# Experts' results scaled at eviction and scattered with a DMA addition into one sum per token

## The reference, cut to what matters

```python
def _hier_moe(h, ..., w_gate, w_up, w_down):
    ...                                     # two experts and two weights for each token
    e_a = expert_id.reshape(-1)             # 4096 assignments
    tok_a = jnp.repeat(jnp.arange(t_count), EXPERT_TOPK)
    w_a = gate_w.reshape(-1)
    ...                                     # sorted by expert, each expert padded to blocks of 128
    slot_tok = jnp.zeros((n_slots,), jnp.int32).at[dest].set(tok_s)
    slot_w = jnp.zeros((n_slots,), h.dtype).at[dest].set(w_s.astype(h.dtype))
    def run_block(args):
        tok, e = args
        xb = h[tok]
        a = xb @ w_gate[e]                  # 1024 x 512
        u = xb @ w_up[e]
        return (jax.nn.silu(a) * u) @ w_down[e]   # 512 x 1024
    y = lax.map(run_block, (slot_tok.reshape(n_blocks, MOE_BLOCK), block_expert))
    y = y.reshape(n_slots, D_MODEL) * slot_w[:, None]
    return jnp.zeros((t_count, D_MODEL), h.dtype).at[slot_tok].add(y)
```

## Time and profile before

| what | value |
|---|---|
| median of three runs | 2801.63 us (2801.57 to 2801.66) |
| profiled execution, its own time | 2803.04 us |
| its span (first to last instruction) | 2801.3 us |
| granted TensorE clock, mean over the span | 0.925 of full |
| busy share of the span | PE 86%, DVE 49%, ACT 33%, POOL 17% |
| moved by DMA | 499.73 MB |
| `combine` stage (first DMA issue to the end of the span) | 2679.11 to 2801.3 us |

### The profile page before, as it was taken

How to read it: one execution, slowest core, us unless ns; L and a number is a source line. 1 busy time by engine, 2 the same in 40 slices (tenths; PEclk the granted TensorE clock), 3 DMA queues, 4 the chain that set the end, 5 groups by cost and what they waited for, 6 DMA issues and landing times. The chain is left out here.

```text
span 2801.3 us, 39203 instructions
## 1 busy us (share of the span) xinstructions
PE 2397.4 (86%) x13485; PEld 2056.7 (73%) x13486; DVE 1365.5 (49%) x1700; ACT 917.5 (33%) x1509; POOL 474.8 (17%) x311
## 2 busy tenths in 40 slices
PE   3599999999999888868959983999999999999910
PEld 3488888888888677846848873888889889889910
DVE  6552111122323177646424447886664756466346
ACT  3200000000000055433322221886664755565321
POOL 2311111111111101022335541010010100010032
PEclk9799999999999999769979995999999999999955
DMA  6112212132332423255554433998975876678468
GB/s 224 46 60 90 75 60 75 60 111 102 132 124 101 162 99 109 81 166 200 200 197 158 151 135 127 368 375 300 323 258 207 289 272 231 240 254 296 184 224 270
DMA packets 293164, 499.73 MB, mean 178 GB/s; under 512 B 21337, under 2 KB 226673, under 8 KB 283506
## 3 DMA queue, kind: packets, MB, share of 16 engines
q1 hardware_dynamic: 269778, 414.05, 43.1%
q0 software_dynamic: 11808, 43.00, 4.6%
q10 hardware_dynamic: 11520, 41.95, 3.8%
HBM read 383.37 MB, written 115.54 MB: 178 GB/s over the span
## 5 line engine op out<-in xcount | busy, mean ns | idle before, releaser
L349 PE MATMUL proj_psum<-h_hi,proj_w_hi 128*128 128x512 f32 x1216 | 481.8, 396 | 19.1 <-POOL proj_w_lo L334 19.1
L350 PE MATMUL proj_psum<-h_lo,proj_w_hi 128*128 128x512 f32 x1216 | 481.6, 396 | 0.0
L351 PE MATMUL proj_psum<-h_hi,proj_w_lo 128*128 128x512 f32 x1216 | 481.4, 396 | 0.0
L1546 PE MATMUL moe_p_gu<-moe_hi_gu,moe_xT_hi 128*128 128x256 f32 x1536 | 440.5, 287 | 1.7 <-DVE moe_xT_lo L1660 1.7
L369 DVE COPY proj_out<-proj_psum 128x512 f32<-128x512 f32 x152 | 123.7, 815 | 635.3 <-PE proj_psum L351 634.1
L1547 PE MATMUL moe_p_gu<-moe_lo_gu,moe_xT_hi 128*128 128x256 f32 x1536 | 432.6, 282 | 0.0
L1548 PE MATMUL moe_p_gu<-moe_hi_gu,moe_xT_lo 128*128 128x256 f32 x1536 | 432.5, 282 | 0.0
L1485 DVE TENSOR_TENSOR moe_lo_gu<-raw_gu,moe_hi_gu 128x1024 fp32r<-128x1024 f32 x256 | 301.5, 1219 | 23.8 <-ACT moe_hi_gu L1479 17.4
L327 ACT ACTIVATE proj_w_hi<-proj_raw 128x1024 fp32r<-128x1024 f32 x38 | 40.3, 1061 | 781.9 <-PE proj_psum L351 772.2
L1546 PEld LDWEIGHTS moe_p_gu<-moe_hi_gu,moe_xT_hi 128*128 128x128 f32 x1536 | 290.5, 189 | 4.2 <-issue 2.1
L1547 PEld LDWEIGHTS moe_p_gu<-moe_lo_gu,moe_xT_hi 128*128 128x128 f32 x1536 | 290.7, 189 | 2.1
(11 more groups left out here) (261 smaller groups left out, 3791.9 us busy)
## 6 DMA issues: line engine op xcount, KB each, us to landing
raw_gu<-in_w_exp_gate SPq DMA_DIRECT2D x256, 256.0 KB, 6.3
raw_gu<-in_w_exp_up SPq DMA_DIRECT2D x256, 256.0 KB, 7.7
raw_d<-in_w_exp_down SPq DMA_DIRECT2D x128, 512.0 KB, 9.1
projected<-proj_out SPq DMA_DIRECT2D x38, 1024.0 KB, 4.3
y_slots<-moe_ys ACTq DMA_DIRECT2D x48, 512.0 KB, 6.4
proj_raw<-in_w_in SPq DMA_DIRECT2D x38, 512.0 KB, 6.2
att_qkv<-projected SPq DMA_DIRECT2D x18, 1024.0 KB, 8.4
proj_w_rest<-in_w_ada SPq DMA_DIRECT2D x8, 2048.0 KB
```

The lines of the kernel that those rows point to most:

```text
L349: pe.matmul(bank, w_hi[:, u, k, :], h_hi[:, k, tok], start=(k == 0), stop=False)
L350: pe.matmul(bank, w_hi[:, u, k, :], h_lo[:, k, tok], start=False, stop=False)
L351: mm = pe.matmul(bank, w_lo[:, u, k, :], h_hi[:, k, tok], start=False, stop=(k == KD - 1))
L1546: pe.matmul(bank, x_hi, w_hi, start=first, stop=False)
```

## The change

- `project` also writes zeros to 20 tiles of 128 rows of a new DRAM tensor `y_sum`, two behind the stores of each of ten turns of SP's loop. DVE clears the source first.
- `route` also finds each slot's weight: ACT multiplies `is_high` by `share`, 32 times 128x64, beside POOL's product with the token's number (now counted from 1); both lie in `value`, and PE's products have 128 columns where they had 64. DVE makes three tensors of `p_rows` where it made one: `slot_rows`, `slot_share` and `slot_place`, which is the token's number, or a row of its own behind the tokens' for a slot without one.
- `experts`: ACT multiplies by the slot's weight in the same instruction that copies `p_y` to `ys`, and issues no store. POOL adds the block to `y_sum` with an indirect DMA that has an addition, waits until it has landed, and only then goes on to the next gather. The zeros for blocks not in use are gone. After the last expert's weights are cut, SP loads 12 of the mixer's 16 tiles into the raw weights' buffers.
- `combine` reads one sum for each token with plain loads, all 16 into buffers of their own, and only four tiles of the mixer. Scaling and adding two rows is gone. All loads are issued ahead of all stores.

```diff
@@ project
+                sp.wait_ge(zeroed, 1)
                 with sp.Fori(1, FIRST_GATE) as j:
                     pair_of_tiles(j)
+                    for u in range(2):
+                        sp.dma_start(y_sum[ds((2 * j + (u - 2)) * P, P), :], zero[:, :]).then_inc(sum_zeroed, 16)
...
@@ route, PE
+                        pe.wait_ge(shares_ready, n // L + 1)
-                    mm = pe.matmul(p_rows[:, 0:NB], is_low[:, n, :], is_high[:, n, :], start=(n == 0), stop=(n == T2 * L - 1))
+                    mm = pe.matmul(p_rows[:, 0:2 * NB], is_low[:, n, :], value[:, n, :], start=(n == 0), stop=(n == T2 * L - 1))
@@ route, ACT
+                for c in range(T2):
+                    act.wait_ge(matched, c + 1)
+                    for t in range(L):
+                        ins = nc.scalar.activation(value[:, c * L + t, NB:2 * NB], is_high[:, c * L + t, :], ACT.Copy,
+                                                   scale=share[:, c, t:t + 1])
+                    ins.then_inc(shares_ready, 1)
@@ route, DVE
-                dve.tensor_copy(slot_rows[:, 0:NB], p_rows[:, 0:NB]).then_inc(rows_ready, 1)
-                dve.wait_ge(rows_ready, 1)
+                dve.tensor_scalar(slot_rows[:, 0:NB], p_rows[:, 0:NB], -1.0, 0.0, ALU.add, ALU.max).then_inc(rows_ready, 1)
+                dve.tensor_copy(slot_share[:, :], p_rows[:, ds(NB, NB)]).then_inc(rows_ready, 1)
+                dve.tensor_copy(found[:, :], p_rows[:, 0:NB]).then_inc(rows_ready, 1)
+                chain.link(dve.tensor_scalar(place[:, :], p_rows[:, 0:NB], 0.0, dummy[:, 0:1], ALU.is_equal, ALU.mult))
+                dve.wait_ge(rows_ready, 3)
+                dve.scalar_tensor_tensor(out=slot_place[:, :], in0=place[:, :], scalar=-1.0, in1=found[:, :],
+                                         op0=ALU.add, op1=ALU.add).then_inc(rows_ready, 1)
@@ experts, SP
-                with sp.Fori(0, NB // 2) as i:
-                    with sp.If(2 * i >= count):
-                        for u in range(2):
-                            sp.dma_start(y_dram[ds((2 * i + u) * P, P), :], zero[:, :]).then_inc(rest_zeroed, 16)
...
+                for g in range(PARTS):
+                    sp.wait_ge(lo_ready[g], cut)
+                    sp.dma_start(x1_part(g, raw_gu, raw_d), x1_dram[ds(g * P, P), :]).then_inc(x1_loaded, 16)
+                sp.wait_ge(x1_loaded, 16 * PARTS)
@@ experts, POOL
+                def scatter(b, u):
+                    pool.tensor_copy(place[:, u:u + 1], slot_place[:, ds(b, 1)]).then_inc(place_ready, 1)
+                    pool.wait_ge(place_ready, b + 1)
+                    pool.wait_ge(y_ready, b + 2)
+                    pool.sem_inc(turn_seen, 1)
+                    pool.indirect_dma_start(out=y_sum, out_offset=bass.IndirectOffsetOnAxis(ap=place[:, u:u + 1], axis=0),
+                                            in_=ys[:, u, :], in_offset=None, compute_op=ALU.add).then_inc(added, 16)
+                    pool.wait_ge(added, 16 * b + 16)
+                    pool.sem_inc(scattered, 1)
+                def block_of(b, u):
+                    gather(b + 2, u)
+                    scatter(b, u)
@@ experts, ACT
-                    act.wait_ge(y_stored[u], 8 * b + (16 - 8 * u))
-                    copy(ys[:, u, :], p_y[:, :, :].rearrange("p a c -> p (a c)")).then_inc(y_ready, 1)
-                    act.wait_ge(y_ready, b + 2)
-                    act.dma_start(y_dram[ds(b * P, P), :], ys[:, u, :]).then_inc(y_stored[u], 16)
+                    act.wait_ge(scattered, b + 1)
+                    nc.scalar.activation(ys[:, u, :], p_y[:, :, :].rearrange("p a c -> p (a c)"), ACT.Copy,
+                                         scale=slot_share[:, ds(b, 1)]).then_inc(y_ready, 1)
@@ combine, SP
+                load_y(0)
                 sp.dma_start(mod[:, :], gate_dram.partition_broadcast(P)).then_inc(mod_loaded, 16)
+                for t in range(1, TILES):
+                    load_y(t)
+                for t in range(LATE):
+                    sp.dma_start(x1[:, t, :], x1_dram[ds((PARTS + t) * P, P), :]).then_inc(x_loaded[t], 16)
...
```

More of the change, by code:

```diff
@@ L254, in _, with project @@
                                       ALU.subtract).then_inc(lo_ready, 1)
-def project(nc, w_in, w_ada, act_c, h_hi, h_lo, proj, ada_part):
+def project(nc, w_in, w_ada, act_c, h_hi, h_lo, proj, ada_part, y_sum):
     FIRST_GATE = GATE_TILE // 2
+    assert SUM_TILES == 2 * (FIRST_GATE - 1)
     assert IN_TILES // 2 - FIRST_GATE == KD
@@ L1215, with x1_part, route @@
 GU, PARTS = 8, 12
-def route(nc, logits, dest, share, table, slot_rows, raw_gu, raw_d, w_gate, w_up, w_down):
+def x1_part(t, raw_gu, raw_d):
+    return raw_gu[:, t, :, :, :].rearrange("p m k f -> p (m k f)") if t < GU else raw_d[:, t - GU, :]
+def route(nc, logits, table, slot_rows, slot_place, slot_share, raw_gu, raw_d, w_gate, w_up, w_down):
     L, T2 = TILES, 2
@@ L1428, in experts @@
         hi_d, lo_d = s.sb("hi_d", [P, KE, D], F32R), s.sb("lo_d", [P, KE, D], F32R)
-        row = s.sb("row", [P, 2], I32)
+        row, place = s.sb("row", [P, 2], I32), s.sb("place", [P, 2], I32)
         xg = s.sb("xg", [P, 2, D])
@@ L1444, in experts @@
         gathered = [s.sem(f"gathered{i}") for i in range(2)]
-        y_stored = [s.sem(f"y_stored{i}") for i in range(2)]
         turned = [s.sem(f"turned{i}") for i in range(2)]
@@ L1644, in _ @@
                         take_x(0, 1)
-                count = by_twos(act, lambda i: [block_of(2 * i, 0), block_of(2 * i + 1, 1)])
-                for u in range(2):
-                    act.wait_ge(y_stored[u], 16 * ((count + 1) >> 1) + 16)
-                    act.sem_inc(all_stored, 1)
+                by_twos(act, lambda i: [block_of(2 * i, 0), block_of(2 * i + 1, 1)])
             @block.vector
@@ L1701, in _, with combine @@
                 by_twos(dve, lambda i: [block_of(2 * i, 0), block_of(2 * i + 1, 1)])
-def combine(nc, dest, share, y_dram, x1_dram, gate_dram, out):
-    BUF = 3
+def combine(nc, y_sum, x1_dram, gate_dram, raw_gu, raw_d, out):
+    LATE = TILES - PARTS
     with ExitStack() as ctx:
         s = Scope(nc, ctx, "comb")
-        yy = s.sb("yy", [P, BUF, 2, D])
-        x1 = s.sb("x1", [P, BUF, D])
-        y = s.sb("y", [P, BUF, D])
-        sq = s.sb("sq", [P, D])
+        y = s.sb("y", [P, TILES, D])
+        x1 = s.sb("x1", [P, LATE, D])
+        sq = s.sb("sq", [P, 2, D])
         mod = s.sb("mod", [P, D])
         eps = s.sb("eps", [P, 1])
-        ms, root, rstd = s.sb("ms", [P, 2]), s.sb("root", [P, 2]), s.sb("rstd", [P, 2])
-        gathered = [s.sem(f"gathered{i}") for i in range(BUF)]
-        x_loaded = [s.sem(f"x_loaded{i}") for i in range(BUF)]
-        stored = [s.sem(f"stored{i}") for i in range(BUF)]
-        mod_loaded, eps_ready, first, mixed, squared, rooted, recips, scaled, summed = (s.sem(n) for n in (
-            "mod_loaded", "eps_ready", "first", "mixed", "squared", "rooted", "recips", "scaled", "summed"))
+        ms, root, rstd = s.sb("ms", [P, TILES]), s.sb("root", [P, TILES]), s.sb("rstd", [P, TILES])
+        y_loaded = [s.sem(f"y_loaded{t}") for t in range(TILES)]
+        x_loaded = [s.sem(f"x_loaded{t}") for t in range(LATE)]
+        mod_loaded, eps_ready, squared, rooted, recips, scaled, summed, stored = (s.sem(n) for n in (
+            "mod_loaded", "eps_ready", "squared", "rooted", "recips", "scaled", "summed", "stored"))
         with nc.Block() as block:
@@ L1801, in build @@
     h_dram = dram("h_moe", (SEQ, D))
-    y_dram = dram("y_slots", (NB * P, D))
+    y_sum = dram("y_sum", (SUM_TILES * P, D))
     with ExitStack() as ctx:
```

115 lines of the change are left out of this document (52 added, 63 removed).

## The result

The changed kernel took 2732.8 us (median of four runs, 2730.6 to 2741.4) against 2801.6 before: ratio 0.976, 95% interval 0.974 to 0.978. The forecast was 2752, its range 2739 to 2790; the time is 6 us under the low end. In three later sets of runs, each on a chip of its own, the same pair gave 0.977 to 0.978.

The account below looks back on a forecast made before the run. It took PE and DMA as both full in the experts, and combine as transfers and waits. 2803.04 - 65.4 (combine) + 7.4 (route) + 6.0 (experts) + 2.7 (tail) = 2753.7, less 1.4 to the median: 2752.3; range 2739 to 2790.

Parts of the forecast that it names:

- Experts: Experts stage: each addition costs DMA 1.33 us more than a store, making eight new experts' weights late; +6.0 us.
- The slack: Experts: an expert's last weights land 4.6 us before ACT needs them, taken off the 10.6 us of piled-up delay.
- Route: Route stage: PE's 64 products, widened to 128 columns, cost +6.6 us and DVE's extra small operations +0.8; +7.4 us.
- The end of 0: Route: lower end for the wider products' cost, 0 us if loading the weights hides the added columns.
- Combine: Combine stage: fewer transfers and less DVE work shorten it from 122.2 to 56.8 us, a gain of 65.4.
- DMA is the later one: 56.8: Combine: 19.4 MB at 361 GB/s makes DMA the limit at 56.8 us, against 54.1 for DVE.
- The new wait: Experts: POOL's wait for an addition's landing (L, taken as 10.1 us) stays hidden, as up to 13.4 us fits.
- rival C: Experts: additions landing later than 13.4 us set every round, making the kernel slower, about 2896 us at 16.4; chance 0.15.
- Tail: End of experts: the last addition lands later than the last store did, so combine begins 2.7 us later.
- Plus 3.9: End of experts: from the last transfer's landing to combine's start takes 3.9 us, as in the kernel before.
- Ahead of route: Stages before route: the 20 stores of zeros in project lie beside PE-bound matmuls and cost 0 us.
- Rival A: Experts: the addition costs DMA no more than a store, its reads hidden beside writes; kernel 2745 us, chance 0.14.

Follow-up runs that it names:

- the changed kernel with its pad: The changed kernel with 32 unused bytes of SBUF ahead of the gathered tokens, moving the turned tokens' address; ratio 0.9826 to the kernel before.
- the kernel before with 128 columns: The kernel before with route's 64 products over 128 columns instead of 64, the added columns unused; ratio 1.0007 to the kernel before.
- the kernels with the late wait: The changed kernel with POOL's wait for an addition moved ahead of the next issue, ratio 0.9769; with early table loads and first gather ahead, 0.9750.
- the plain scatter: The changed kernel with each block's indirect addition turned into a scatter without addition (output wrong); ratio 0.9761 to the kernel before.

## Why the prediction was wrong

The direction, the stage and the reason of the gain were right. The forecast change of -49.3 us misses the measured -69.4 by 20.1. Experts was 13.2 us too dear, route 8.6, the stretch ahead of route 3.1, combine 2.8, and the tail was 7.5 too cheap.

- **Experts** (forecast +6.0, measured -7.2). Two steps failed. The first is a term that was not there: new tensors shift addresses, and that was worth 9.5 to 10 us in the kernel before and 9 to 12 in the changed one. Without it the time would have lain inside the range. The second is the step from "6.0 us late" to "Experts: +6.0 us". With the addresses of the kernel before (the changed kernel with its pad) the seven late rounds took 142.9 us instead of 137.7, 5.2 late. But the next round, in which no weights are due, gave 3.2 back (13.3 instead of 16.5), and the ninth lost 1.0: 178.7 us against 175.6 for nine rounds, +3.1. The addition's price was right (1.6 us of the engines more than a plain scatter, against 1.33 forecast), and so was the place where it shows: waits for weights from the third or fourth round of the eight on, none in the runs of three.
- **The slack** (4.6 us) was misread, as shown under the addition's cost: it was 3.0. With that the forecast's own sum would have been 10.6 - 3.0 = 7.6 us late, further from the 5.2.
- **Route** (forecast +7.4, measured -1.2). This step fell altogether: "both rows are at half clock, so a column costs 1.6 ns". Two measured sizes, 64 and 512 columns, gave a slope, but the price is flat from 64 to 128 columns. The end of 0 that the step named ("if loading the weights hides the columns") was the right one, and the clock's rise went below it. DVE's own chain is last now; its five operations cost the +0.8 as forecast (49.1 us against 48.3 in the kernel before with 128 columns).
- **Combine** (forecast -65.4, measured -68.2). DVE's limit was worked out at 54.1 us, the stage took 54.0. What failed is "DMA is the later one: 56.8": the 361 GB/s of the earlier trace rows came from a stretch of gathers beside one broadcast, and plain loads and stores ran at 408 to 419. The share of 0.91 looks like the forecast's "above 0.9", but DVE's row, without a pause, shows which of the two is the limit.
- **The new wait** (hidden, L 10.1). Additions landed in 6.1 to 11.2 us, so rival C's condition, more than 13.4, was not met. But the wait was not free: behind the late rounds the gather came late too, and the ninth round took 22.3 to 22.6 us where the kernels with the late wait have 21.0 to 21.2.
- **Tail** (forecast +2.7, measured +10.2). The landing of the last addition was mis-sized by little (6.2 against 5.4), and so was the start of its issue (0.8 us behind the eviction, not 0.1). "Plus 3.9" failed: it was taken as the price of a barrier from the kernel before, where POOL's last transfer was long past. With an indirect transfer as POOL's last work its idle turns (3.8) and its drain (4.9) lie behind the landing.
- **Ahead of route** (0, measured -3.1): within what this stretch scatters.

Without the accident of the addresses the number would have looked right. The changed kernel with its pad has a ratio of 0.9826, which on 2801.6 is 2753 us, where 2752 was forecast. That would have been luck: route too dear by 8.6 and the tail too cheap by 7.5 nearly cancel. Rival A named the nearest time (2745), and that is luck too: the plain scatter refutes its reason, the addition is not as cheap as a store.

## What to carry to other kernels

A slope through two sizes of an instruction holds only between sizes that have the same limit; look for a third row, or keep both ends in the range. Before a run of late rounds is added up, look at the round behind it: one with time to spare gives a part back. When a change adds or removes a tensor, compare the addresses of PE's operands before trusting that untouched stages keep their time. Where a stage ends in a barrier, ask what each engine's last instruction is: a wait that is free in the loop, and POOL's drain, come to stand on the path there.

## What the runs showed of the hardware

- PE's pace in products of 256 columns, each with its own stationary operand: 0.1134 to 0.1138 us in some blocks and 0.1178 in the others with the operand at remainder 0 by 64 bytes of SBUF, 0.1173 to 0.1186 in all but the first at 32; 9 to 12 us over 48 blocks.
- f32 products of route: 0.213 us at half clock for 64 and 128 columns alike, 0.320 for 192.
- An indirect addition of 128 rows of 4 KB: 1.6 us of the 16 DMA engines more than a plain scatter, landing unloaded 6.2 us against 3.3.
- POOL's drain at the end of the experts, behind its last indirect transfer: 4.2 us in the kernel before, off the path, and 4.9 to 8.1 in the changed kernel and its variants, on it.
- 408 to 419 GB/s in a stage of plain loads and stores, where the first 10 us of a stage with gathers ran at 361.
- A DVE instruction with two inputs in SBUF beside a POOL addition: 3.39 us instead of 1.28.
